# Reading the moving operand backwards, and moving the split activations by 256 bytes

## The reference, cut to what matters

```python
def swiglu(h, wg, wu, wd):
    return (jax.nn.silu(h @ wg) * (h @ wu)) @ wd      # 1024 -> 2816 -> 1024
...
for l in range(DEPTH):                                 # DEPTH = 2
    h = modulate(x, 0)
    x = x + 0.5 * gate(0) * swiglu(h, ffn_wg[l, 0], ffn_wu[l, 0], ffn_wd[l, 0])
    h = modulate(x, 1)
    z = h @ w_in[l]                                    # 1024 -> 6400
    q, k, v, u, gates = jnp.split(z, SPLITS, axis=-1)
    ...
    y = jax.nn.sigmoid(g_attn) * y_attn + jax.nn.sigmoid(g_conv) * y_conv
    x = x + gate(1) * (y @ w_out[l])
    h = modulate(x, 2)
    x = x + 0.5 * gate(2) * swiglu(h, ffn_wg[l, 1], ffn_wu[l, 1], ffn_wd[l, 1])
return rms_norm(x, final_g)
```

## Time and profile before

| | |
|---|---|
| median of the runs | 1296.92 us |
| span of the profiled execution, first to last instruction | 1293.5 us |
| PE (TensorE matmul) busy | 1238.3 us, 96%, 5448 matmuls |
| PEld (weight load) busy | 957.3 us, 74%, 5448 loads |
| DVE (VectorE) busy | 965.1 us, 75% |
| ACT (ScalarE) busy | 547.3 us, 42% |
| mean granted TensorE clock | 0.994 of full speed |
| DMA | 293.44 MB, mean 227 GB/s |

### The profile page before, as it was taken

The page is one execution under the profiler, slowest core; times in us unless marked ns, Lnnn a source line. Parts: engine busy times, 40 slices in busy tenths (PEclk is TensorE's granted clock), DMA queues, the critical chain, the costliest instruction groups (busy, mean ns, idle before and its releaser), DMA issues.

```text
span 1293.5 us, 13852 instructions
## 1 busy us (share of the span) xinstructions
PE 1238.3 (96%) x5448; PEld 957.3 (74%) x5448; DVE 965.1 (75%) x1341; ACT 547.3 (42%) x576; POOL 2.2 (0%) x5
## 2 busy tenths in 40 slices
PE   3999999999998999999999999999999899999997
PEld 2588887765765787888878888876676677888885
DVE  5698886699996576988668888669999856744443
ACT  3353344532345365344354443354233454644331
POOL 0000000000000000000000000000000000000000
PEclk9999999999999999999999999999999899999999
DMA  9989994454323339889747899454432334555540
GB/s 374 417 316 378 372 377 169 163 183 159 130 98 130 137 124 376 340 340 358 294 180 280 340 343 357 174 188 174 175 130 98 130 130 169 190 190 178 204 177 33
DMA packets 52913, 293.44 MB, mean 227 GB/s; under 512 B 6640, under 2 KB 6896, under 8 KB 27120
## 3 DMA queue, kind: packets, MB, share of 16 engines
q1 hardware_dynamic: 51120, 289.38, 60.0%
q10 hardware_dynamic: 1728, 3.17, 0.7%
HBM read 291.45 MB, written 1.07 MB: 226 GB/s over the span
## 4 chain that ended last, share of the span: by engine, by line
PE 89%; DVE 4%; DMA 3%; ACT 2%; issue 1%; SPq 0%; DVEq 0%
PE ps L329 23%; PE ps L331 23%; PE ps L330 23%; PE ps L348 13%; DMA raw<-in_weights 2%; PE ps L537 1%; PE ps L515 1%; PE ps L396 1%; DMA ada_raw<-in_ada_w 1%; DVE w_lo L997 1%; DVE hF L1084 1%; PE ps L526 0%; PE ps L485 0%; ACT L714 0%; DVE hA_lo L997 0%
## 5 line engine op out<-in xcount | busy, mean ns | idle before, releaser
L997 DVE TENSOR_TENSOR w_lo<-raw,w_hi 128x2048 fp32r<-128x2048 f32 x176 | 401.1, 2287 | 37.6 <-ACT w_hi L708 37.3
L708 ACT CAST w_hi<-raw 128x2048 fp32r<-128x2048 f32 x176 | 334.5, 1910 | 176.8 <-DMA raw<-in_weights 113.7
L329 PE MATMUL ps<-w_hi,hA_hi 128*128 128x512 f32 (+1 forms) x992 | 395.9, 399 | 5.8 <-DVE hA_lo L997 5.8
L331 PE MATMUL ps<-w_hi,hA_lo 128*128 128x512 f32 (+1 forms) x992 | 384.3, 387 | 0.0
L330 PE MATMUL ps<-w_lo,hA_hi 128*128 128x512 f32 (+1 forms) x992 | 383.6, 387 | 0.0
L329 PEld LDWEIGHTS ps<-w_hi,hA_hi 128*128 128x128 f32 x992 | 186.9, 188 | 49.8 <-issue 15.1
L331 PEld LDWEIGHTS ps<-w_hi,hA_lo 128*128 128x128 f32 x992 | 186.7, 188 | 39.0
L330 PEld LDWEIGHTS ps<-w_lo,hA_hi 128*128 128x128 f32 x992 | 187.0, 189 | 37.9 <-issue 2.9
L1186 DVE SCALAR_TENSOR_TENSOR work<-conv_in,par,work 128x256 f32<-128x256 f32 x480 | 193.9, 483 | 0.0
L1012 DVE SCALAR_TENSOR_TENSOR product<-ada_raw,c_bc 128x1024 f32<-128x1024 f32 x144 | 171.7, 1220 | 16.0 <-DMA ada_raw<-in_ada_w 15.6
L348 PE MATMUL ps<-raw,hF 128*128 128x512 f32 x384 | 172.0, 600 | 5.5 <-ACT hF L733 5.5
(11 more groups left out here) (121 smaller groups left out, 749.7 us busy)
## 6 DMA issues: line engine op xcount, KB each, us to landing
raw<-in_weights SPq DMA_DIRECT2D x200, 1024.0 KB, 4.9
ada_raw<-in_ada_w SPq DMA_DIRECT2D x144, 512.0 KB, 7.5
gate_bc<-gate_scratch ACTq DMA_DIRECT2D x6, 512.0 KB, 6.4
x<-in_x_tok SPq DMA_DIRECT2D x1, 1024.0 KB, 7.6
out_tok<-xn_h SPq DMA_DIRECT2D x4, 256.0 KB, 2.2
c_bc<-in_c_row SPq DMA_DIRECT2D x1, 512.0 KB, 4.6
c_bc<-in_g_row SPq DMA_DIRECT2D x1, 512.0 KB, 5.6
mask_all<-in_mask SPq DMA_DIRECT2D x1, 416.0 KB, 16.6
```

The source lines that it names most:

```text
L329: nc.tensor.matmul(out_ap, stat[0], mov[0], start=start, stop=False)
L331: return nc.tensor.matmul(out_ap, stat[1], mov[0], start=False, stop=stop)
L708: nc.scalar.copy(w_hi[:, s % HI, :], raw[:, p % RAW, :]).then_inc(hi_done, 1)
L997: return nc.vector.tensor_tensor(dst, whole, hi_part.bitcast(F32), ALU.subtract)
```

## The change

Each moving operand that is a slice of a weight panel is read from its last column to its first (step -1). The host reverses the columns inside each chunk beforehand (512 wide, 256 wide in the one panel that `v1` reads), so that the products and their order in PSUM are the same. The split activations, and all that shares their regions, get the remainder 256 instead of 0. `hF` stays at 0 and the weight slots stay where they are. No instruction is added, removed or moved on any engine. In the compiled programs, before and after, each weight load walks its 128 columns from the last to the first, with step -1; the compiler writes it that way.

```diff
-        hA_at = room(2 * KC * T * 4, 0)
+        hA_at = room(2 * KC * T * 4, 256)
...
-        att_at = room(16896, 0)
+        att_at = room(16896, 256)
...
-        gates_at = room(16384, 0)
+        gates_at = room(16384, 256)
...
+            def back(first, n):
+                return slice(first + n - 1, first - 1 if first else None, -1)
...
                 for i in range(4):                                    # k_half
-                    k, c = 4 * b + i, slice(512 * i, 512 * i + 512)
+                    k, c = 4 * b + i, back(512 * i, 512)
...
                     for kk in range(2):                               # two_chunks
-                        c = slice(kk * D + half * 512, kk * D + half * 512 + 512)
+                        c = back(kk * D + half * 512, 512)
...
                     for k in range(KC):                               # v1
-                        c = slice(k * 256, k * 256 + 256)
+                        c = back(k * 256, 256)
...
-    weights = np.stack(panels)
+    narrow = [mix_base(l) + M_V1 for l in range(DEPTH)]
+    weights = np.stack([w.reshape(P, -1, 256 if p in narrow else 512)[:, :, ::-1].reshape(P, PW)
+                        for p, w in enumerate(panels)])
```

## The result

| | before | changed |
|---|---|---|
| median of the runs | 1296.91 us | 1319.01 us |
| span of the profiled execution | 1293.5 us | 1316.4 us |

The changed kernel is slower by 1.8%: the ratio is 1.0177, with a 95% interval of 1.0161 to 1.0193. The 1319 us lie inside the range of 1248 to 1358 us, but the forecast was 1265 us and faster.

A forecast was written before the change was run, and what follows sets the result against it. It took TensorE as the bound, mostly split matmuls at 228.3 ns. Terms of -34.2 us (fewer meetings) and +2 us (loads) gave -32.2: span 1261.3 us, plus 3.4 for the median, rounded to 1265 us; range 1248 to 1358 us.

The forecast's parts named there:

- What bounds the kernel, and the unit: TensorE, busy 1238.3 of 1293.5 us, bounds the kernel; split matmuls are costed by distance between starts, 228.3 ns each.
- The 12.3 ns: Part of each split matmul's 228.3 ns beyond the 216.0 ns it could cost, taken as time the moving walk loses.
- The 12.3 ns as meetings of two walks: In split matmuls, moving and weight reads lose 12.3 ns where they meet in SBUF: three rounds opposed, one in the same direction.
- the yardstick of 216.0: Possible split matmul cost in ns: 213.3 for 512 columns plus the 2.7 read from whole matmuls.
- the term was -34.2 us: Backward moving read in 4176 split matmuls: 228.3 to 220.1 ns each, 8.2 ns less.
- "caught" rival: Moving walk held behind the weight walk in split matmuls: 242.7 ns each, 60 us more, 1357 us; chance 0.22.
- The offset: Split activations' 256 bytes decide where the one meeting falls: 0 to 17 us either way, nothing added.
- The first nine matmuls: After a pause in TensorE's stream, nine took 232.2 ns each, then six 226.7; read as two streams' relative timing.
- The narrow matmuls: The 96 split matmuls of 256 columns: possible gain 0.8 to 1.2 us, taken as 0.
- Whole matmuls, other engines, loads: Whole matmuls keep 429 ns a record, VectorE and ScalarE stay hidden, both 0; waiting on loads takes back 2 us.
- No change: Rival: split matmuls' 12.3 ns is a fixed cost of the fp32r form, so nothing meets; 1297 us; chance 0.10.
- half rate: Rival: backward columns in split matmuls come at half pace; 2137 us, up to 2302 with whole ones; chance 0.11.

The follow-up runs named there:

- e3: Kernel before, forward read, with stationary remainders set to 128 for hA, 64 for hB and o, 384 for mid and end: 1318.8 us.
- e8: Kernel before, forward read, with stationary remainders set to 32 for hA, 192 for hB and o, 160 for mid and end: 1318.5 us.
- e17: Kernel before, forward read, with high and low halves of hA, hB and mid interleaved, so weight loads take every second column: 1319.9 us, ratio 1.0190.
- e10: Changed kernel, backward read, remainder 0, stationary operands of 64 columns instead of 128 except in trios opening or closing an accumulation: 1319.6 us.
- e1: Changed kernel with the offset undone, split activations at remainder 0, backward read kept: 1317.86 us, ratio 1.0172 to the kernel before.
- e2: Kernel before with the offset alone, split activations at remainder 256, forward read kept: 1295.58 us, ratio 0.9995.
- e18: Kernel before with columns read backward inside blocks of 16 (64 bytes), blocks in ascending order: 1449.6 us.
- e14: Kernel before with columns read backward inside blocks of 4 (16 bytes), blocks in ascending order: 1296.5 us.
- e5: Kernel before with blocks of 64 columns (256 bytes) taken from last to first, each read forward: 1296.4 us.
- e13: Kernel before with all tiles moved up together by 128 bytes, forward read: 1296.3 us.
- e9: Kernel before, forward read, stationary operands of 64 columns instead of 128 except in trios opening or closing an accumulation: 1304.4 us.
- e15: Changed kernel, backward, remainder 0; 256 moving and 64 stationary columns except in trios opening or closing an accumulation: 117.9 ns between short-loaded matmuls; no run time given.
- e20: Kernel before, forward; 256 moving and 64 stationary columns except in trios opening or closing an accumulation: 114.7 ns between short-loaded matmuls; no run time given.

## Why the prediction was wrong

- *What bounds the kernel, and the unit.* Right. TensorE's busy time took the whole difference, a matmul is counted by the distance between starts, and 5.92 ns x 4176 = 24.7 us accounts for the 22.9 us of the span.
- *The 12.3 ns.* The size is a little high. The window of the earlier trace rows holds 814 matmuls, of which the working names 806; the other 8 are transposes, and the mean distance in the trace is 227.46 ns, not 228.3. A split matmul's own share is 11.5 ns.
- *The 12.3 ns as meetings of two walks.* Half right. That the stationary side's address and layout change the distance forward (`e3`, `e8`, `e17`) shows that the two reads do act on each other. The pace taken for the weight walk fits too: with 64 columns less, its records are 53 ns shorter (188 to 135 ns in `e10`), which makes 107 for 128. But the lost time does not count meetings.
- *The failed step: "If what is lost goes with the number of meetings modulo 512 bytes, a third of 12.3 ns stays".* Backward a settled split matmul stands 17.3 ns over the yardstick of 216.0, where 4.1 should have stayed. Over the bare 213.3 ns that is a loss of 20.0, against 13.3 in the kernel before. It is 20.0 too with loads of half the length (`e10`), which by the prediction's count have half a round of meetings in place of one, and at all eight remainders tried, so that it does not matter where the meeting falls. Forward it is 20.0 too, on average, at most remainders. Of all arrangements tried, the old one, opposite directions and aligned, has the smallest loss, 13.3 ns settled. I read the even 226.7 ns as the ordinary price that another direction might lower. It is a favourable case that the kernel before happens to stand in, and the change left it. The sign was wrong for that reason; the term was -34.2 us and measured about +25 (5.92 ns x 4176). That the measured time lies in the range all the same is luck: the range reached so high only for the "caught" rival, whose mechanism is not there either.
- *The offset.* I allowed 17 us either way and added nothing. It is worth nothing, forward and backward (`e1`, `e2`), because 256 is a period of the effect.
- *The first nine matmuls.* The 232.2 ns are one stretch. Over all streams of the kernel before, the first nine distances average 230.0 ns, from 232 at the start to 228 at the ninth. They showed that 226.7 is not the only pace; I used them only to argue that something varies, and did not ask whether 226.7 was the exception.
- *The narrow matmuls.* I put them at 0. They measured -1.5 ns each, 0.1 us over all.
- *Whole matmuls, other engines, loads.* Right: 429.3 to 429.4 ns a record in both kernels, and no more than 429.5 in any run, `e18` included, the busy times of VectorE and ScalarE unchanged, and the loads a little less in the way.
- *The rivals.* "No change" was refuted, and "half rate" as well. "Caught behind the weight walk" had the right sign, but its 242.7 ns and its mechanism are not what is there: a held walk would go on for less time behind a load of half the length, and `e10` has the same 233.3.

The Trainium skill, "SBUF — State Buffer", section "Who interferes with whom", gives TensorE two independent read ports, one for the moving operand and one for the weight load, and says that it never waits on anyone. The runs don't bear out that the two reads are without effect on each other: for the split matmuls, `e3` and `e17` change only where and how the stationary activations lie, and that costs 6.5 to 7.3 ns a matmul. The Trainium skill, "SBUF — State Buffer", section "Door 1: The DMA port swizzle", has lines of 16 bytes inside which consecutive reads run at full rate. `e14`, which turns the order inside each 16 bytes and stays at 226.7 ns, agrees.

Open is why the loss is 20.0 ns backward and 13.3 forward. No split matmul can be made here without its weight load, so it is not shown whether a moving walk alone would have it. That it goes with the columns and, backward, ignores address and length of the load speaks for the moving walk by itself; that is argued, not shown. No run turns the weight walk, so it is not shown either that its direction matters. Open too are the half exception at 192 bytes and the 266.7 ns of `e18`. No version beat the kernel before: `e2`, `e5`, `e13` and `e14` stand level with it.

## What to carry to other kernels

Before changing how an operand is read, ask whether the present distance between matmuls is the normal price or a favourable exception; shifting one operand by 128 bytes, as `e3` does, is a cheap way to find out. For fp32r streams of 512 columns with a weight load of 128 columns beside each matmul, keep stationary blocks and moving chunks at the same address modulo 256 bytes and read forward: 226.7 ns in place of 233.3, 22 us in this kernel. With 256 columns nothing was gained by it. And try the two parts of a two-part change apart before believing the story that joins them.

## What the runs showed that was not expected

- Forward, remainders 0 and 256 cost the same (`e2`), and so do 128 and 384, where the prediction counted in rounds of 512 bytes. It is the distance between moving and stationary operand that counts, not their place in SBUF (`e13`).
- The order of the columns between 16 and 256 bytes sets the rate: ascending 226.7 ns, descending inside 256 bytes 233.3, descending inside 64 bytes 266.7 (1449.6 us). The whole matmuls, whose columns are read in the same order in all these runs, keep 429.3 ns.
- Matmuls of 256 columns with full loads lose 13.3 ns forward, as much as those of 512, and 11.7 backward, where those of 512 lose 20.0.
- Shorter weight loads can cost time: forward, 64 stationary columns in place of 128 raised the distance from 226.7 to 229.8 ns (`e9`).
- With over a third of TensorE's columns left out (`e15`, `e20`), TensorE waited more (busy 84% and 83% of the span, against 96%), the mean granted clock fell to 0.935 and 0.940, and for stretches matmuls of 256 columns stood 213 ns apart, the lower level of 1.2 GHz.
